# Gate and up products of a mixture-of-experts kernel as two halves of columns, even and odd, each with its own PSUM bank

## What is computed

```
# t: (384, 1024); 32 experts in 4 groups; top-1 group, then top-2 experts inside it
a = einsum('nd,edf->nef', t, w_gate)          # w_gate, w_up: (32, 1024, 256)
u = einsum('nd,edf->nef', t, w_up)
act = silu(a) * u * combine[..., None]
y = einsum('nef,efd->nd', act, w_down)        # w_down: (32, 256, 1024)
```

## Time and profile before

| | |
|---|---|
| runs, us | 967.51, 968.96, 969.69; median 968.96 |
| the profiled execution: its own time, us | 970.48 |
| its span, first to last instruction, us | 968.7 |
| mean granted TensorE clock | 0.956 |
| TensorE busy | 843.2 us, 87% of the span |
| VectorE, ScalarE, GpSimd busy | 341.3, 156.5, 162.3 us |
| DMA | 317.24 MB, mean 327 GB/s |

### The profile page before, as it was taken

The page is one execution under the profiler, slowest core; times in us unless marked ns, Lnnn a source line. Parts: engine busy times, 40 slices in busy tenths (PEclk is TensorE's granted clock), DMA queues, the critical chain, the costliest instruction groups (busy, mean ns, idle before and its releaser), DMA issues. The chain is left out here.

```text
span 968.7 us, 12779 instructions
## 1 busy us (share of the span) xinstructions
PE 843.2 (87%) x4927; PEld 429.2 (44%) x4927; DVE 341.3 (35%) x818; ACT 156.5 (16%) x355; POOL 162.3 (17%) x188
## 2 busy tenths in 40 slices
PE   3889999998898898999888788999699988888883
PEld 3556666655548533333333335556533333333331
DVE  3113454556586311111110128948611111111036
ACT  0122222223200101111110112001111111111013
POOL 2041212113121202111101100223111101010100
PEclk9999999999996899999999999999599999999897
DMA  9998393539427897999999979976879999999971
GB/s 332 365 373 305 121 385 123 177 108 363 152 84 289 343 408 324 383 420 417 419 419 419 418 314 376 392 275 220 355 315 419 419 419 419 420 419 419 420 291 65
DMA packets 90012, 317.24 MB, mean 327 GB/s; under 512 B 12686, under 2 KB 25710, under 8 KB 65864
## 3 DMA queue, kind: packets, MB, share of 16 engines
q1 hardware_dynamic: 74400, 289.41, 75.8%
q0 software_dynamic: 12256, 19.78, 5.9%
q10 hardware_dynamic: 3272, 6.91, 1.9%
HBM read 309.46 MB, written 28.90 MB: 349 GB/s over the span
## 5 line engine op out<-in xcount | busy, mean ns | idle before, releaser
L1083 PE MATMUL psum<-ring,arena 128*64 128x512 f32 x880 | 255.2, 624 | 28.6 <-DMA ring<-in_w_expert_up 16.6
L1083 PEld LDWEIGHTS psum<-ring,arena 128*64 128x64 f32 x880 | 85.4, 144 | 157.4 <-issue 154.2
L1105 PE MATMUL psum<-ring,arena 128*64 128x512 f32 x440 | 124.2, 599 | 16.6 <-DVE arena L1925 15.9
L1921 DVE TENSOR_TENSOR arena<-arena,psum 128x256 f32<-128x256 f32 x34 | 14.3, 421 | 271.7 <-ACT arena L1436 271.7
L1083 PE MATMUL psum<-h_hT,arena 128*64 128x512 f32 x208 | 97.9, 627 | 4.5 <-DMA ring<-in_w_expert_up 3.6
L953 PE MATMUL psum<-ring,h_hT 128*128 128x384 f32 x288 | 98.0, 495 | 0.0
L697 POOL DMA_INDIRECT y_scratch<-arena,table x30 | 30.8, 1026 | 355.1 <-DVE arena L1931 343.5
L899 PE MATMUL psum<-ring,h_hT 128*128 128x512 f32 x160 | 69.3, 594 | 1.8 <-ACT h_hT L1531 1.5
L953 PEld LDWEIGHTS psum<-ring,h_hT 128*128 128x128 f32 x288 | 54.5, 194 | 34.8 <-issue 1.6
L1105 PEld LDWEIGHTS psum<-ring,arena 128*64 128x64 f32 x440 | 35.7, 137 | 67.8 <-issue 46.9
L1931 DVE COPY arena<-psum 128x512 f32<-128x512 f32 x32 | 22.1, 692 | 120.5 <-PE psum L1105 120.5
(11 more groups left out here) (236 smaller groups left out, 914.8 us busy)
## 6 DMA issues: line engine op xcount, KB each, us to landing
ring<-in_w_expert_down SPq DMA_DIRECT2D x52, 1024.0 KB, 21.4
ring<-in_w_expert_gate SPq DMA_DIRECT2D x50, 1024.0 KB, 19.5
ring<-in_w_expert_up SPq DMA_DIRECT2D x50, 1024.0 KB, 21.9
ring<-in_w_ada SPq DMA_DIRECT2D x24, 2048.0 KB, 14.8
h_hT<-in_w_expert_gate SPq DMA_DIRECT2D x12, 1024.0 KB, 19.6
h_hT<-in_w_expert_up SPq DMA_DIRECT2D x12, 1024.0 KB, 22.6
h_hT<-in_w_expert_down SPq DMA_DIRECT2D x12, 1024.0 KB, 24.6
ring<-in_w_qkv SPq DMA_DIRECT2D x9, 1024.0 KB, 12.5
```

Of the source, the lines that this page charges most:

```text
L1083: last = pe.matmul(bank[b][64 * e:64 * e + 64, :].rearrange("p (g n) -> p g n", g=2), mem.GT[b][:, c, 64 * e:64 * e + 64], w, start=(c == ...
L1105: last = pe.matmul(bank[5 + half][64 * e:64 * e + 64, :], mem.actT[b][:, f, 64 * e:64 * e + 64], w[:, f, 512 * half:512 * half + 512], sta ...
L1921: V.tensor_tensor(mem.act[b], mem.sil[b], bank[b][:, FE:2 * FE], ALU.mult).then_inc(S["act"], 1)
```

## The change

`gate_up` no longer makes 512 columns at a time. The columns f of an expert are taken as even (f = 0) and odd (f = 1). A first half makes the even gate and the even up columns for all eight chunks, 128 and 128 of them, into bank 0; a second half makes the odd ones into bank 1. The moving operand reads every second float. The number of matmuls doubles (64 instructions for 32) and each is half as wide (256 for 512). SiLU, the multiplication, the transpose and the eviction are each done by half: two instructions of half the width instead of one.

On TensorE the transpose of the first half (`act_transpose(S, 2 * k, 0)`) stands inside the second half's products, before their last two chunks. The transpose of the second half stands inside `down`, whose products now come in the order (bank 5, even), transpose, (bank 6, even), wait for the odd half, (bank 5, odd), (bank 6, odd). Pair 15 makes both halves of chunks 0 to 3, waits, makes the rest, and then transposes. VectorE's order becomes up_times 0, at_evict 0, up_times 1, gt_evict(n + 1), at_evict 1.

`u_ps` now counts two per pass, and SyncE waits for the second. The spread vectors move from pairs 4 to 11 to pairs 6 to 13.

```diff
-        self.sil = [view(16 + b, FE) for b in range(2)]
-        self.act = [view(18 + b, FE) for b in range(2)]
+        self.sil = [view(16 + f, FE // 2) for f in range(2)]
+        self.act = [view(18 + f, FE // 2) for f in range(2)]
...
-        FIRST_SPREAD, VECTORS = 4, 8
+        FIRST_SPREAD, VECTORS = 6, 8
...
-                        sp.wait_ge(main[l]["u_ps"], n + 1)
+                        sp.wait_ge(main[l]["u_ps"], 2 * n + 2)
...
-            def gate_up(S, k, n, b, landings, rest=()):
+            def gate_up_chunks(n, b, f, chunks):
+
+                for c in chunks:
+                    for e in range(2):
+                        w = mem.slot(2 * n + e)[:, 0:4 * D].rearrange("p (g k d f) -> p g k d f", g=2, k=KC, f=2)[:, :, c, :, f]
+                        last = pe.matmul(bank[f][64 * e:64 * e + 64, 0:FE].rearrange("p (g n) -> p g n", g=2),
+                                         mem.GT[b][:, c, 64 * e:64 * e + 64], w,
+                                         start=(c == 0), stop=(c == KC - 1))
+                return last
...
+            def gate_up(S, k, n, b, landings):
+
+                rows_turned(S, k)
                 for done, value in landings:
                     pe.wait_ge(done, value)
...
+                gate_up_chunks(n, b, 0, range(KC)).then_inc(S["u_ps"], 1)
+                gate_up_chunks(n, b, 1, range(0, KC - 2))
+                act_transpose(S, 2 * k, 0)
+                gate_up_chunks(n, b, 1, range(KC - 2, KC)).then_inc(S["u_ps"], 1)
+
+            def gate_up_halves(S, k, n, b, landings, rest):
...
+                for f in range(2):
+                    gate_up_chunks(n, b, f, range(0, KC // 2))
+                for done, value in rest:
+                    pe.wait_ge(done, value)
+                for f in range(2):
+                    gate_up_chunks(n, b, f, range(KC // 2, KC)).then_inc(S["u_ps"], 1)
+                act_transpose(S, 2 * k, 0)
+
+            def act_transpose(S, k2, f):
+
+                done = k2 + f + 1
+                pe.wait_ge(S["act"], done if isinstance(done, int) else pe.snap(done))
+                pe.transpose(bank[4][:, P * f:P * f + P], mem.act[f], ident).then_inc(S["at_ps"], 1)
...
+                product(0, 0)
+                act_transpose(S, 2 * k, 1)
+                product(1, 0)
+                pe.wait_ge(S["at_sb"], second if isinstance(second, int) else pe.snap(second))
+                product(0, 1)
+                product(1, 1).then_inc(S["d_ps"], 1)
...
-            def silu(S, n, b):
-                act.wait_ge(S["u_ps"], n + 1)
-                nc.scalar.activation(mem.sil[b], bank[b][:, 0:FE], ACT.Silu).then_inc(S["sil"], 1)
+            def silu(S, n):
+                for f in range(2):
+                    done = 2 * n + f + 1
+                    act.wait_ge(S["u_ps"], done if isinstance(done, int) else act.snap(done))
+                    nc.scalar.activation(mem.sil[f], bank[f][:, 0:FE // 2], ACT.Silu).then_inc(S["sil"], 1)
...
-                    up_times(S, n, b)
+                    up_times(S, n, 0)
                     if n < LAST:
+                        at_evict(S, n, b, 0)
+                        up_times(S, n, 1)
                         gt_evict(S, n + 1, 1 - b)
-                    at_evict(S, n, b)
+                    else:
+                        up_times(S, n, 1)
+                        at_evict(S, n, b, 0)
+                    at_evict(S, n, b, 1)
...
                     gt_evict(extra, k, b)
-                    up_times(extra, k, b)
+                    up_times(extra, k, 0)
+                    at_evict(extra, k, b, 0)
+                    up_times(extra, k, 1)
                     dve.sem_inc(gate_up_through, 1)
-                    at_evict(extra, k, b)
+                    at_evict(extra, k, b, 1)
```

More of the change, by code:

```diff
@@ L1073, in gate_up, with rows_turned @@
+            def rows_turned(S, k):
                 pe.wait_ge(S["gt_act"], k + 1)
                 pe.wait_ge(S["gt_dve"], k + 1)
+            def gate_up(S, k, n, b, landings):
+                rows_turned(S, k)
                 for done, value in landings:
                     pe.wait_ge(done, value)
[L1077 to L1085 removed]
@@ L1086, in gate_up @@
-                last.then_inc(S["u_ps"], 1)
-            def act_transposes(S, n, b):
-                pe.wait_ge(S["act"], n + 1)
-                for f in range(2):
-                    last = pe.transpose(bank[4][:, P * f:P * f + P],
-                                        mem.act[b].rearrange("p (d f) -> p f d", f=2)[:, f, :], ident)
-                last.then_inc(S["at_ps"], 1)
-            def down(S, k, n, b, landings):
-                pe.wait_ge(S["at_sb"], k + 1)
+                gate_up_chunks(n, b, 0, range(KC)).then_inc(S["u_ps"], 1)
@@ new lines, in act_transpose, with down, product @@
+            def act_transpose(S, k2, f):
+                done = k2 + f + 1
+                pe.wait_ge(S["act"], done if isinstance(done, int) else pe.snap(done))
+                pe.transpose(bank[4][:, P * f:P * f + P], mem.act[f], ident).then_inc(S["at_ps"], 1)
+            def down(S, k, n, b, landings):
+                def product(half, f):
+                    for e in range(2):
+                        w = mem.slot(2 * n + e)[:, 4 * D:].rearrange("p (k n) -> p k n", k=2)
+                        last = pe.matmul(bank[5 + half][64 * e:64 * e + 64, :],
+                                         mem.actT[b][:, f, 64 * e:64 * e + 64],
+                                         w[:, f, 512 * half:512 * half + 512], start=(f == 0), stop=(f == 1))
+                    return last
+                first, second = 2 * k + 1, 2 * k + 2
+                pe.wait_ge(S["at_sb"], first if isinstance(first, int) else pe.snap(first))
@@ L1100, in down @@
                 pe.wait_ge(S["o_dve"], k + 1)
-                for half in range(2):
-                    for f in range(2):
-                        for e in range(2):
-                            w = mem.slot(2 * n + e)[:, 4 * D:].rearrange("p (k n) -> p k n", k=2)
-                            last = pe.matmul(bank[5 + half][64 * e:64 * e + 64, :],
-                                             mem.actT[b][:, f, 64 * e:64 * e + 64],
-                                             w[:, f, 512 * half:512 * half + 512], start=(f == 0), stop=(f == 1))
-                last.then_inc(S["d_ps"], 1)
+                product(0, 0)
[4 more added lines that the diff above has]
+                product(1, 1).then_inc(S["d_ps"], 1)
             def mlp(l):
@@ L1481, in first @@
                 def first(n, b):
-                    silu(S, n, b)
+                    silu(S, n)
                     if n < LAST:
```

40 lines of the change are left out of this document (18 added, 22 removed).

## The result

The median of the changed kernel is 972.46 us (970.68 to 977.58, 20 runs), of the kernel before 969.64 us (967.11 to 973.11, 20 runs): ratio 1.0033, 95% interval 1.0021 to 1.0045. **The change costs 3.2 us** by the ratio (the two medians are 2.8 us apart); forecast were 2.3 us less and a range of 964.3 to 971.0, and 972.46 lies above it. The profiled execution has a span of 972.6 us against 968.7.

What follows compares the result with a forecast made beforehand. Weight DMA was taken to bound mid-stages, leaving four stretches that count: -2.3 - 0.25 + 0.35 - 0.25 = -2.45, with 0.15 back for gathers, -2.3 us. Forecast 966.7 us, range 964.3 to 971.0.

Steps and rivals of the forecast that it cites:

- What bounds the kernel: Both expert stages: weights at 419 GB/s set mid-stage length; only each layer's start to its dry-DMA load and its end count.
- Half-width products: Gate and up: 32 rounds of 256 columns instead of 16 of 512 cost 0.05 us more per pass.
- the 80-column row: Profile row with two tiles reading every second float: 142 ns a round against 133, taken as upper bound, 0.3 us a pass.
- The inserted transpose: Twice a pass, in gate and up and in down: 0.32 us each, bounds 0.13 and 0.46.
- The wait before down: Between gt and down: 1.27 us shrinks to 0.10, so an ordinary pass gains 0.5 us.
- The further pass: Pass without a gt to hide behind: down begins at once after gate and up, gaining 1.5 us.
- Layer 0 to 388.02: Layer 0 from its first pass to the load issued at 388.02: that load comes 2.3 us earlier.
- Ends and layer 1: Layer ends: -0.25 us each from pair 14, nothing from pair 15; layer 1's load at 710.89 moves +0.35.
- The spread vectors: Moved to pairs 6 to 13: some 1.2 us per pair, hidden by 2.8 us that weights leave; cost nothing.
- the slower side: Whole kernel: slower than before by over 0.2%, chance 0.17.
- the second rival: Gate and up: weight loads bound short rounds, 240 ns instead of 213; +3.6 us, 972.6; slower, chance 0.17.
- The clock rival: Longer waits before landings halve the clock, costing up to 2.5 us in layer 1's pair 14; part of no change, 0.33.

Runs made afterwards that it cites:

- full_width_strided: Kernel before, matmuls still 512 wide and as many, but reading every second float (even gate, odd gate, even up, odd up); ratio to before 0.9984.
- padded_before: Kernel before with 64 never-executed transposes written into TensorE's stream ahead of pair 15, behind a condition that is never true; ratio to before 1.0023.
- short_end_after: Changed kernel without TensorE's further-pass code in pairs 14 and 15 of layer 1; ratio to the kernel before 0.9993.
- turns_beside_gt: Changed kernel with both transposes moved beside the next pair's gt, none inside an ordinary pair's products; ratio to the kernel before 1.0009.
- contig_halves: Changed kernel with halves as columns 0 to 127 and 128 to 255, down weights loaded in 4 KB pieces; ratio to the kernel before 1.0028.
- even_odd_alone: Kernel before with even and odd columns made one after the other, 256 wide, reading every second float, all else as before; ratio to before 1.0038.
- gate_then_up: Kernel before with gate, then up, each in 32 rounds of 256 neighbouring columns, nothing inserted; ratio to before 1.0013.
- short_before: Kernel before without TensorE's code for a further pass in layer 1; ratio to before 1.0000.

## Why the prediction was wrong

*What bounds the kernel*: right. The stretches with full-rate stages keep their length to within some 3 us over all kernels, and the load at 388.02 and the end of layer 1 are where the differences of this account lie. The stretch from pair 14 to layer 1 scatters as much (142.5 to 146.2 us), in no relation to the kernel.

*Half-width products*: the width was right (0.04 us a pass, predicted 0.05). The term was mis-sized by the stride: 227 - 216 = 11 ns a round, 0.35 us a pass, of which contiguous halves leave 0.04. The upper bound, 9 ns from the 80-column row with the same reading, came near it, and the prediction took the lower rows because they were nearer in width. The property that mattered was how they read. That the bound came so near is partly luck: it was carried over as 9 ns a round, from 80 columns at a granted clock of 0.50, while the price turned out to be per column.

*The inserted transpose*: 0.32 us predicted, 0.355 measured. The Trainium skill ("TensorEngine Tiling (Array Packing)", Key Properties) says that a change of tiling mode drains the array; 0.23 us around a transpose of 0.126 agree with that, and the prediction's upper bound with the way out exposed in full, 0.46 us, was not seen.

*The wait before down*: predicted -1.27 + 0.10, gt to down went from 2.28 to 1.09. Right. With the true prices an ordinary pass gains 1.19 - 2 x 0.355 - 0.35 = 0.13 us instead of 0.5; from the first pass to the further pass's products both kernels have 14.9.

*The further pass*: 1.1 us instead of 1.5, by the stride again.

*Layer 0 to 388.02*: **this is the forecast term that failed by most, 2.3 us forecast and 0.6 measured.** With 1.1 from the further pass and nothing from pairs 0 and 1, pair 2's second gather and the further pass's gt move by 1.2 us, not 2.5 (379.3 - 326.04 against 378.34 - 323.85), and the gate and up before the load are 0.7 us longer, not 0.32. What is left is 0.6 us.

*Ends and layer 1*: **the forecast of -0.25 for layer 1's end had the wrong sign: it is 1.1 and 2.6 us longer in the two profiles of the changed kernel.** It took TensorE as ready when pair 15's weights land. No step of the sum and no rival counted instructions as something that has to arrive. An "issue" of this kind was there to read, in the timeline of the kernel before, ahead of pair 15 in layer 0:

```profile
572.46 7.09 PE L1083 MATMUL psum<-ring,arena 128*64 128x512 f32 x32 [1.36 <-issue]
```

That VectorE's at_evict 1 and ScalarE's SiLU stand ahead of the row sums in program order was priced at nothing, which holds only while pair 15 is in time. For layer 1's restart +0.35 was forecast; the first load came 711.22 - 701.76 = 9.46 us after the pass began (before 9.62), but SyncE's next issues took 1.47 and 1.14 us (0.43 each in layer 0), and DMA ran at 329 GB/s from 715 to 720. From layer 1's first pass to pair 14 the kernels before take 213.0 to 213.8, the changed one 214.6 and 213.8.

*The spread vectors* cost nothing visible, as forecast.

*Rivals*: the slower side came true with almost the time that the second rival gave (972.6), but by luck and not by its mechanism. Its point of decision, 10 ns a round, was even reached, by the stride and not by the weight load; full_width_strided, as strided and not slower, shows that it did not decide. The clock rival did happen, in pair 15 rather than 14, and in one of the two profiles.

*What stays open*: the size. The end explains 1.1 to 2.6 us of 3.2, against the 53.6 of the kernel before (in two other profiles of its order, 55.0 and 55.1, pair 14 itself ran at the lower clock, 9.9 to 10.0 us, which costs as much), and the profiles scatter by some us ahead of the first pass (319.0 to 326.0, in no relation to the kernel), so the sum by stages can't be closed within 1 us. That late code has a part in the loss is shown, by padded_before and short_end_after; how large its part is beside the insertions is not, since turns_beside_gt got rid of most of the loss and kept the late start. Why some first loads of layer 1 are issued slowly is open too: a packet of instructions lands beside them, 10 to 12 us after the pass began, in five profiles of the changed order (at 14.6 us and later elsewhere, but for one at 4.8 us in padded_before), but in two of these, contig_halves and short_end_after, DMA ran at full rate.

## What to carry to other kernels

An instruction stream has a length, and a jump over code that does not run is not free: where the profile shows idle time "issue" ahead of a group, look at the instruction queue's packets, and count what a change adds to the program of the engine that must not be late. Doubling the matmuls of a loop that is written out sixteen times can cost more than their slower columns do: even_odd_alone and full_width_strided read the same columns, and 0.5% lie between them. A bound for a new access should come from the row that shares the access, not from the one that shares the size. And before splitting work to hide a wait, try the order of the engine that makes the wait: one moved line took 0.25 us from a pass and measured 0.24% faster, about what was forecast for the whole split, though the interval is barely clear of no change.

## What the runs showed of the hardware

- **Reading every second float as moving operand** costs 5% per column: 227 ns instead of 216 to 218 for 256 columns, 7.41 us instead of 7.09 for 512-column products.
- **Instruction fetch**: packets of 16 KB; TensorE goes on 1.6 to 1.7 us after the packet has landed (930.85 to 932.57 in the changed kernel, 929.78 to 931.42 in its second run, 928.80 to 930.44 in gate_then_up; 2.0 us in padded_before, 933.34 to 935.38), and idled up to 3.35 us ahead of it. The same engine order with two further passes less in the code has none of it.
- **The clock after a wait**: after 3.27 us of idle time the next 64 matmuls took 9.04 us in one execution and 7.43 in the next, at the same place (3.35 us idle). It is not certain from run to run, and 1.6 us hang on it. Ahead of pair 14 the same is seen with waits for a landing: after 3.57 us of idle time in short_before its 32 matmuls took 9.97 us, after 0.75 us in the kernel before 7.09.
